# Normalisation, residual and first-projection steps of a three-layer hybrid kernel rearranged

## The reference

```
h = rms_norm(x, g_norm);  proj = h @ w_in              # RWKV-7 scan, conv, memory attention
y = gates0*y_rwkv + gates1*y_conv + gates2*y_mem
x = rms_norm(x + y @ w_out, g_final)
for layer in range(2):
    h = rms_norm(x, norm_pre[layer]);  proj = h @ w_in_2[layer]
    y = concat(gla(...), diff_attention(...), hgrn(...)) @ w_out_2[layer]
    x = x + rms_norm(y, norm_post[layer])
# rms_norm(x, g) = x * rsqrt(mean over channels of x*x, plus 1e-6) * g
```

## Time and profile before

| | us |
|---|---|
| median of three runs | 4637.75 (4632.31 to 4640.51) |
| the profiled execution | 4640.63, its span 4638.7 |
| PE busy | 3902.2 (84%) |
| DVE busy | 2036.1 (44%) |
| ACT busy | 1438.2 (31%) |
| POOL busy | 1007.3 (22%) |

### The profile page before, as it was taken

One profiled execution on the slowest core, in us unless ns is written; L12 is line 12 of the kernel. 1 busy time (PEld: TensorE's weight loads), 2 busy tenths in 40 slices (PEclk: granted clock), 3 DMA queues, 4 the chain that ended last, 5 costly groups with the idle time before them and its releaser, 6 DMA issues.

```text
span 4638.7 us, 66428 instructions
## 1 busy us (share of the span) xinstructions
PE 3902.2 (84%) x29046; PEld 2418.3 (52%) x29346; DVE 2036.1 (44%) x2160; ACT 1438.2 (31%) x1794; POOL 1007.3 (22%) x442
## 2 busy tenths in 40 slices
PE   5988899999989999777995977979685877978776
PEld 2555565665656654345443555555452455555443
DVE  3456455455444551412224254263734254264642
ACT  4222323323233221311113323434443232343442
POOL 2313333233332321111131101111023200111013
PEclk9999999999999999888997988989897978989888
DMA  2111111111111113223222100100011100100011
GB/s 89 51 38 38 52 38 47 47 51 52 38 51 38 51 65 141 77 95 114 104 69 74 33 10 9 42 14 28 19 59 61 33 10 10 41 19 19 23 50 55
DMA packets 61585, 226.93 MB, mean 49 GB/s; under 512 B 6832, under 2 KB 8560, under 8 KB 60784
## 3 DMA queue, kind: packets, MB, share of 16 engines
q1 hardware_dynamic: 50064, 181.77, 11.3%
q10 hardware_dynamic: 11232, 40.90, 2.2%
HBM read 174.93 MB, written 47.71 MB: 48 GB/s over the span
## 4 chain that ended last, share of the span: by engine, by line
PE 68%; DVE 17%; ACT 10%; issue 2%; POOL 2%; DMA 1%; ACTq 0%; DVEq 0%; SPq 0%; POOLq 0%
PE psum L886 66%; DVE arena L1925 6%; ACT arena L1419 6%; DVE arena L1928 5%; DVE arena L2355 2%; DVE arena L2292 2%; POOL arena L2401 2%; PE psum L889 1%; ACT L1419 1%; DVE arena L1932 1%; ACT hh L1419 1%; ACT wh L1419 1%; ACT arena L1866 1%; DVE hl L1925 1%; POOL wl L2401 0%
## 5 line engine op out<-in xcount | busy, mean ns | idle before, releaser
L886 PE MATMUL psum<-arena 64*64 64x32 f32 (+12 forms) x19058 | 1595.4, 284 | 505.9 <-DVE arena L1925 199.8
L886 PEld LDWEIGHTS psum<-arena 64*64 64x64 f32 (+6 forms) x19058 | 1114.5, 160 | 994.4 <-issue 512.3
L2401 POOL TENSOR_TENSOR wl<-arena,wh 128x1024 bf16<-128x1024 f32 (+1 forms) x195 | 474.7, 2435 | 2436.2 <-ACT wh L1419 2434.2
L886 PE MATMUL psum<-hh,wh 128*128 128x512 f32 x3120 | 890.3, 432 | 121.8 <-ACT hh L1419 72.9
L1419 ACT ACTIVATE arena<-psum 128x512 f32<-128x512 f32 (+4 forms) x660 | 415.8, 630 | 1242.5 <-PE psum L886 960.2
L886 PEld LDWEIGHTS psum<-hh,wh 128*128 128x128 f32 x3120 | 609.0, 201 | 330.6 <-ACT hh L1419 85.1
L1925 DVE TENSOR_TENSOR arena<-psum,arena 128x512 f32<-128x512 f32 (+3 forms) x488 | 319.4, 654 | 980.0 <-PE psum L886 635.1
L886 PE MATMUL psum<-hh,wl 128*128 128x512 bf16 (+1 forms) x2911 | 727.9, 392 | 20.7 <-issue 7.4
L886 PE MATMUL psum<-hl,wh 128*128 128x512 bf16 (+1 forms) x3029 | 717.6, 383 | 10.6 <-issue 8.1
L1928 DVE SCALAR_TENSOR_TENSOR arena<-arena 128x1024 f32<-128x1024 f32 (+1 forms) x388 | 610.1, 1572 | 118.4 <-ACT arena L1419 103.4
L1925 DVE TENSOR_TENSOR arena<-arena 128x1024 f32<-128x1024 f32 (+9 forms) x514 | 434.3, 845 | 371.2 <-ACT arena L1419 209.2
(11 more groups left out here) (30 smaller groups left out, 819.5 us busy)
## 6 DMA issues: line engine op xcount, KB each, us to landing
arena<-in_w_in SPq DMA_DIRECT2D x161, 512.0 KB, 3.5
scr_g<-arena ACTq DMA_DIRECT2D x24, 512.0 KB, 2.6
arena<-scr_g SPq DMA_DIRECT2D x24, 512.0 KB, 4.6
arena<-in_w_out SPq DMA_DIRECT2D x24, 512.0 KB, 3.5
arena<-in_w_mem_kv SPq DMA_DIRECT2D x16, 512.0 KB, 3.5
scr_x<-arena SPq DMA_DIRECT2D x16, 512.0 KB, 2.6
arena<-scr_x SPq DMA_DIRECT2D x16, 512.0 KB, 7.3
arena<-in_x SPq DMA_DIRECT2D x8, 512.0 KB, 10.3
```

Source lines behind the costliest of these rows:

```text
L886: return pe.e.matmul(o, l, r, start=start, stop=stop)
L2401: return pool.seq.tensor_tensor(o, a, b, op)
```

## The change

- The inverse root of every norm stays in PSUM: Ln and Exp work in place on the statistics' pair of banks, and DVE reads it there. The pair is given back by the last norm (or the last residual multiplication), not by Ln.
- `stat_sum`: PE multiplies the sum of the first seven slices by ones, then the eighth's squares by ones into the same banks. The last `stat_add` is gone and four passes are added. For `pre1` there is no `stat_add`: PE sums every slice's squares (`stat_mm`).
- `resid`: DVE multiplies all eight slices; DVE adds the even ones and POOL the odd ones. For layer 0 it runs inside the `pre1` statistics, and `stat_sq` k waits for slice k alone.
- `ahead_by_two`: the plan says norm k, then split k-2; `norm_pre` has four rotating buffers.
- In `post0`/`post1` `stat_sq` comes ahead of `close`, and `close` gives back the projection's banks.
- The low parts of `m0` and `m1` are all made by DVE.
- The first projections named in `EARLY` go slice by slice: for each k the two high x high matmuls and the two with the weights' low part, and at the end the 16 with the activations' low part.

```diff
@@ stat, ahead_by_two (plan)
         for k in range(8):
+            if tag == "pre1":
+                do("resid", 0, k)
             do("stat_sq", tag, k)
-            if k:
+            if tag == "pre1":
+                do("stat_mm", tag, k)
+            elif 0 < k < 7:
                 do("stat_add", tag, k)
             yield
-        do("stat_sum", tag)
-        ps.leave(("stat", tag))
+        if tag != "pre1":
+            do("stat_sum", tag)
         do("stat_end", tag)
+    def ahead_by_two(norms, tag):
+        for k in range(10):
+            if k < 8:
+                do(*norms[k])
+            if k > 1:
+                do("split", tag, k - 2)
-    for k in range(8):
-        do("norm_x", k)
-        do("split", "h", k)
+    ahead_by_two([("norm_x", k) for k in range(8)], "h")
+    ps.leave(("stat", "x"))
@@ closing (plan)
-            do("close", tag, ct)
+            if tag == "fin":
+                do("close", tag, ct)
             do("stat_sq", tag, ct)
-            if ct:
+            if 0 < ct < 7:
                 do("stat_add", tag, ct)
+            if tag != "fin":
+                do("close", tag, ct)
@@ the two layers (plan)
-        for k in range(8):
-            do("norm_pre", L, k)
-            do("split", f"p{L}", k)
+        ahead_by_two([("norm_pre", L, k) for k in range(8)], f"p{L}")
+        ps.leave(("stat", f"pre{L}"))
...
-        for ct in range(NT):
-            do("resid", L, ct)
+    for ct in range(NT):
+        do("resid", 1, ct)
@@ PE
+    EARLY = [("lo", 0), ("m", 1, 0), ("fin", 0)]
+    EARLY += [("dvp", 0, 0), ("sv", 0, 0, 0), ("post0", 0), ("dvp", 1, 0), ("sv", 1, 0, 0), ("post1", 0)]
+    def lo_by_dve(tag, k):
+        return 1 if tag[0] == "m" else k % 2
-                kind, c0, k = q // each, q % each // 8 * 512, q % 8
+                if key in EARLY:
+                    kind, c0, k = (q % 4 // 2, q % 2 * 512, q // 4) if q < 32 else (2, q % 2 * 512, q % 16 // 2)
+                else:
+                    kind, c0, k = q // each, q % each // 8 * 512, q % 8
@@ PE, stat_sum
-            pe.wait_ge(*at("stat_add", tag, 7))
+            pe.wait_ge(*at("stat_add", tag, 6))
             for c in range(0, n, 512):
                 e = min(n, c + 512)
-                x = mm(o[:, c:e], ones, stat_acc(tag)[:, c:e])
+                mm(o[:, c:e], ones, stat_acc(tag)[:, c:e], True, False)
+            pe.wait_ge(*at("stat_sq", tag, 7))
+            for c in range(0, n, 512):
+                e = min(n, c + 512)
+                x = mm(o[:, c:e], ones, STAT[tag][2][1][:, c:e], False, True)
             x.then_inc(*pe.up("stat_sum", tag))
+        def stat_mm(tag, k):
+            pe.wait_ge(*at("stat_sq", tag, k))
+            src = STAT[tag][2][k % 2] if k else stat_acc(tag)
+            for c in (0, 512):
+                x = mm(o[:, c:c + 512], ones, src[:, c:c + 512], k == 0, k == 7)
@@ ACT
             elif tag == "pre1":
-                act.wait_ge(*at("resid_pool", 0, 7))
-                act.wait_ge(*at("resid_dve", 0, 6))
+                act.wait_ge(*at(("resid_dve", "resid_pool")[k % 2], 0, k))
-            f(rs[:, 0:n], pair(("stat", tag))[:, 0:n], AF.Ln, bias=EPS6, scale=1.0 / D).then_inc(*act.up("stat_ln", tag))
-            ps.give(("stat", tag), ("stat_ln", tag))
-            f(rs[:, 0:n], rs[:, 0:n], AF.Exp, scale=-0.5).then_inc(*act.up("stat", tag))
+            f(inv_root(tag), inv_root(tag), AF.Ln, bias=EPS6, scale=1.0 / D).then_inc(*act.up("stat_ln", tag))
+            f(inv_root(tag), inv_root(tag), AF.Exp, scale=-0.5).then_inc(*act.up("stat", tag))
@@ DVE (norm_x, mem_norm and norm_fin alike)
-            if k > 1:
-                dve.wait_ge(*ready_h(f"p{L}", k - 2))
-            stt(sl(1024 * (k % 2), 1024), XR[:, k, :], V("norm_pre_2", 8 * L + k), STAT[f"pre{L}"][3], MUL, MUL).then_inc(*dve.up("norm_pre", L, k))
+            if k > 3:
+                dve.wait_ge(*ready_h(f"p{L}", k - 4))
+            stt(sl(1024 * (k % 4), 1024), XR[:, k, :], V("norm_pre_2", 8 * L + k), inv_root(f"pre{L}"), MUL, MUL).then_inc(*dve.up("norm_pre", L, k))
+            if k == 7:
+                ps.give(("stat", f"pre{L}"), ("norm_pre", L, 7))
         def resid(L, ct):
+            dve.wait_ge(*at("stat", f"post{L}"))
+            dve.wait_ge(*at("close", f"post{L}", ct))
+            tt(BB[:, ct, :], BB[:, ct, :], inv_root(f"post{L}"), MUL).then_inc(*dve.up("resid_mul", L, ct))
             if ct % 2 == 0:
                 dve.wait_ge(*at("xr_in", L))
                 tt(XR[:, ct, :], XR[:, ct, :], BB[:, ct, :], ADD).then_inc(*dve.up("resid_dve", L, ct))
@@ POOL
             if ct % 2:
-                pool.wait_ge(*at("stat", f"post{L}"))
                 pool.wait_ge(*at("xr_in", L))
-                tt(BB[:, ct, :], BB[:, ct, :], STAT[f"post{L}"][3], MUL).then_inc(*pool.up("resid_mul_pool", L, ct))
+                pool.wait_ge(*at("resid_mul", L, ct))
                 tt(XR[:, ct, :], XR[:, ct, :], BB[:, ct, :], ADD).then_inc(*pool.up("resid_pool", L, ct))
```

More of the change, by code:

```diff
@@ L573, in memory @@
         do("mem_norm")
+        ps.leave(("stat", "mem"))
         for ct in range(8):
@@ L828, in build @@
     for stage, names in (
-            ("weights", "load proj split"), ("stat", "stat_sq stat_add stat_sum stat_end norm_x norm_fin norm_pre close resid"),
+            ("weights", "load proj split"), ("stat", "stat_sq stat_add stat_mm stat_sum stat_end norm_x norm_fin norm_pre close resid"),
             ("keys", "init shift lo_tanh ksq ksum kn kn2 lora_load lora lsig cs kh rkh bsum powers bon ar bk"),
@@ L1338, in do_sum @@
             sums(("do_sum", L, h), "sums", ones, PX)
-        does = dict(proj=proj, vmp=vmp, stat_sum=stat_sum, ksum=ksum, lora=lora, bsum=bsum, G=g_mats, vt=vt, sx=sx, sp=sp,
+        does = dict(proj=proj, vmp=vmp, stat_sum=stat_sum, stat_mm=stat_mm, ksum=ksum, lora=lora, bsum=bsum, G=g_mats, vt=vt, sx=sx, sp=sp,
                     sq=sq, ta=ta, bt=bt, w0=w0, tu=tu, mr=mr, dd=dd, y0=y0, ch=ch_step, ys=ys, gmean=gmean, gvar=gvar, usum=usum, usqs=usqs, ms=ms, mt=mt,
@@ L1368, in stat_acc, with inv_root @@
         return acc[:, 0:n]
+    def inv_root(tag):
+        return pair(("stat", tag))[:, 0:STAT[tag][0]]
     final = {}
@@ L1383, in split_src @@
         if tag[0] == "p":
-            return sl(1024 * (k % 2), 1024)
+            return sl(1024 * (k % 4), 1024)
         return BA[:, k, :]
@@ L1455, in stat_sq @@
             if k > 2:
-                act.wait_ge(*at("stat_add", tag, k - 2))
+                act.wait_ge(*at("stat_mm" if tag == "pre1" else "stat_add", tag, k - 2))
             elif tag == "mem":
@@ L1715, in close @@
             f(BB[:, ct, :], pair(("proj", (tag, ct))), AF.Copy, scale=V("norm_post_2", 8 * L + ct)).then_inc(*act.up("close", tag, ct))
+            ps.give(("proj", (tag, ct)), ("close", tag, ct))
         def small(L):
@@ L1949, in norm_x @@
             dve.wait_ge(*at("stat", "x"))
-            stt(BC[:, k, :], BC[:, k, :], V("g_norm", k), STAT["x"][3], MUL, MUL).then_inc(*dve.up("norm_x", k))
+            stt(BC[:, k, :], BC[:, k, :], V("g_norm", k), inv_root("x"), MUL, MUL).then_inc(*dve.up("norm_x", k))
+            if k == 7:
+                ps.give(("stat", "x"), ("norm_x", 7))
         def split(tag, k):
-            if k % 2:
+            if lo_by_dve(tag, k):
                 dve.wait_ge(*at("hi", tag, k))
@@ L2174, in mem_norm @@
             for k in range(8):
-                x = stt(MT[:, k, :], MT[:, k, :], V("g_mem_norm", k), STAT["mem"][3], MUL, MUL)
+                x = stt(MT[:, k, :], MT[:, k, :], V("g_mem_norm", k), inv_root("mem"), MUL, MUL)
                 x.then_inc(*(dve.up("mem_norm") if k == 7 else dve.up("mem_norm", k)))
+            ps.give(("stat", "mem"), ("mem_norm",))
         def ms(h, b):
@@ L2207, in norm_fin @@
             dve.wait_ge(*at("stat", "fin"))
-            stt(BC[:, ct, :], BC[:, ct, :], V("g_final", ct), STAT["fin"][3], MUL, MUL).then_inc(*dve.up("norm_fin", ct))
+            stt(BC[:, ct, :], BC[:, ct, :], V("g_final", ct), inv_root("fin"), MUL, MUL).then_inc(*dve.up("norm_fin", ct))
+            if ct == 7:
+                ps.give(("stat", "fin"), ("norm_fin", 7))
         def norm_pre(L, k):
             dve.wait_ge(*at("stat", f"pre{L}"))
-            if k > 1:
-                dve.wait_ge(*ready_h(f"p{L}", k - 2))
-            stt(sl(1024 * (k % 2), 1024), XR[:, k, :], V("norm_pre_2", 8 * L + k), STAT[f"pre{L}"][3], MUL, MUL).then_inc(*dve.up("norm_pre", L, k))
+            if k > 3:
+                dve.wait_ge(*ready_h(f"p{L}", k - 4))
+            stt(sl(1024 * (k % 4), 1024), XR[:, k, :], V("norm_pre_2", 8 * L + k), inv_root(f"pre{L}"), MUL, MUL).then_inc(*dve.up("norm_pre", L, k))
+            if k == 7:
+                ps.give(("stat", f"pre{L}"), ("norm_pre", L, 7))
         def small(L):
@@ L2414, in split @@
         def split(tag, k):
-            if k % 2 == 0:
+            if not lo_by_dve(tag, k):
                 pool.wait_ge(*at("hi", tag, k))
```

13 lines of the change are left out of this document (7 added, 6 removed).

## The result

The changed kernel takes 4565.24 us (median of four runs, 4556.62 to 4578.9); the kernel before took 4635.95 (4632.31 to 4640.51) beside it. The ratio is 0.985, 95% interval 0.9822 to 0.9877: faster by 1.2 to 1.8%. The forecast was 4576.0, range 4558 to 4594. Twice more beside other kernels it gave 4578.58 (ratio 0.9868, 0.9836 to 0.9899) and 4571.33 (0.9859, 0.9838 to 0.9879). One execution in this document, of the kernel with `EARLY` off, took 5922.55 us at a granted clock of 0.632 and is left out of that kernel's median and ratio.

A forecast was written before the change was run, and what follows sets the result against it. PE was taken as the bound, with the gain in the seams where it waits for vector work. Terms from +1.7 to -20.9 us summed to -61.7, off the median 4637.75: 4576.0 us, range 4558 to 4594.

The forecast's parts named there:

- Start: First norm-and-split stretch: Ln of x +1.5 us later, then first norm to the end of `lo` -8.2 us.
- rival C: `p0` and `p1`: low parts, not high ones, end last, so the gain is 2 us each; 4583 us, chance 0.10.
- the bound on cooling: fin's first tile: -0.5 us, bounds -1.5 to +2, since waits between low parts may cool PE.
- `p0`, `p1`: Layers' projections after the first norm: end at 38.1 us against 43.5, -5.4 us each, bounds -3.4 to -9.
- The new wait on n7: `p0` and `p1`: PE stands at `sv`'s first matmul until the eighth norm returns the statistics' PSUM pair, at 17.0 us.
- Rivals A: Start, `p0`, `p1`, residuals: much milder stretching, eighth norm at 13 us; about -17 us, 4559 us, chance 0.13.
- `m0`, `m1`: Layers' closings: 20 matmuls instead of 41 after the eighth high part, DVE's low parts just in time; -6.2 us each.
- The weight DMAs: `m0` and `m1`: costed at nothing; a late DMA at the third tile would give back 4 us.
- One of the prediction's own signs of being wrong: `m0`: PE matmuls showing 0.45 us each would mean the prediction is wrong.
- Residual, `pre1`, end: From `post0` through the residual to Ln of `pre1`, -20.9 us; the end of the kernel, -9.1 us.
- Rival B: Thin stretches: PE stays at half clock; `pre1` sums +7 us, `m0` and `m1` +4 each; 4593 us, chance 0.12.
- Rival D: Steady parts: PE fills its gaps and is granted less clock; 2% gives 4654 us, slower than before; chance 0.02.

The follow-up runs named there:

- the kernel with the norms ahead: Changed kernel with all eight norms ahead of all splits on DVE, each in its own buffer: 4551.19 us, ratio 0.9813 to the kernel before.
- run 32: Not a run or kernel: in "let PE run 32 matmuls" the word run is a verb and 32 counts matmuls.
- The upper half: Changed kernel with the sums of `pre0` and `pre1` in the upper half of PSUM, so `sv` needs no pair from it: 4558.45 us, ratio 0.9827.
- the three edits together: Changed kernel with `pre0`/`pre1` sums in upper PSUM, low parts of y on DVE alone, all norms ahead of splits: 4531.72 us, ratio 0.9789.
- the last two runs: The changed kernel with upper-PSUM sums, y low parts on DVE and norms ahead, 4531.72 us; and the changed kernel unedited a third time, 4571.33 us.

## Why the prediction was right

**What bounds it, and that the seams pay in full.** Right. PE's busy time stayed, and -59.5 of -61.6 us lie in the seams, -59.8 of -58.4 and -60.2 of -64.5 in the two repeats.

**Start.** The sum was +1.3 for +1.5. n7 ended 17.1 after the first norm for 17.0, the eighth high part 18.2 for 18.1, from the rule that a low part that meets POOL's ends 1.08 after it. Of the tail the prediction took the middle between 4.6 us at the fast and 9 at the slow clock. PE ran the last 20 matmuls from 49.12 to 55.86 without a wait, 6.7 us; the granted clock was 0.50 to 0.52 until 53.3 and 1.00 from there. So the size (-7.8 for -8.2) and the reason were right. DVE's last two low parts, stretched, end at 54.40, and PE comes to the eighth slice's only at 55.26: rival C's mechanism, low parts that end last, has 0.9 us to spare here, and the kernel with the norms ahead shows it in `lo`.

```profile
45.22 2.60 DVE L1968 SCALAR_TENSOR_TENSOR arena<-arena,psum 128x1024 f32<-128x1024 f32 x2
47.92 6.48 DVE L1965 TENSOR_TENSOR hl<-arena,hh 128x1024 bf16<-128x1024 f32 x2
...
49.18 1.42 PE L909 MATMUL psum<-hh,wh 128*128 128x512 f32 x2
50.40 1.08 PE L909 MATMUL psum<-hh,wl 128*128 128x512 bf16 x2
51.27 4.59 PE L909 MATMUL psum<-hl,wh 128*128 128x512 bf16 x15
...
55.90 1.11 ACT L1463 ACTIVATE arena<-psum,arena 128x1024 f32<-128x1024 f32 x1 [5.84 <-PE psum L909]
```

**fin.** The first tile and the sum were right. The step that failed is the bound on cooling, "-1.5 to +2" counted for the first tile alone: PE's waits for POOL's low parts, the longest 2.24 us, slow the second tile too, which the earlier trace rows didn't show. The granted clock was 1.00 until 2390, 0.50 from 2392.3 to 2401.1 and 0.97 after. These rows tell it, sixteen matmuls in 6.21 where the third tile's take 4.01:

```profile
2392.32 1.89 PE L909 MATMUL psum<-hl,wh 128*128 128x512 bf16 x4 [2.24 <-POOL hl L2451]
2395.60 1.89 PE L909 MATMUL psum<-hl,wh 128*128 128x512 bf16 x4 [1.39 <-POOL hl L2451]
2396.93 6.21 PE L909 MATMUL psum<-hh,wh 128*128 128x512 f32 x16
```

So `EARLY` loses 1.5 us at fin, +2.0 - 0.5, where the kernel without it shows both the old times. The loss isn't steady: the changed kernel's two repeats lose 0.2 and 1.0. In the first of them PE's waits are the same to 0.01 us, but the clock is back at 1.00 about 3 us sooner. The old order let PE run 32 matmuls of the other products while POOL finished.

**`p0`, `p1`.** The new wait on n7 was found, with its length: PE goes on at 17.3 for 17.0 and needs 21.4 for 21.1. The upper half took it away and gave 20.1 in the time. Of the 0.8 that is missing in `p0`, 0.23 is an edge ('s window is 43.5, the stretch by instructions 43.27), 0.27 the later n7 and 0.3 the tail. Rivals A and C did not come: the low parts s1 and s3 took 3.20 and 3.18 us, and n7 ended at 17.2, not 13; the low parts end 21.9 us after the first norm and hold nothing.

**`m0`, `m1`.** -6.07 and -6.08 for -6.2. Both halves were needed: the order alone, with POOL's share back, loses 3.9 and 2.5; the old order loses 6.0. The weight DMAs that were costed at nothing cost nothing. One of the prediction's own signs of being wrong did appear, matmuls at 0.43 us in `m0`: the granted clock was 0.53 from 3429.4 to 3432.6, behind PE's wait of 2.35 us for the first high part. It cost little: a high part came only every 1.1 us, and PE reached the eighth slice 0.5 us after its high part.

**Residual, `pre1`, end.** -21.5 for -20.9 and -9.3 for -9.1. Rival B's clock didn't come: the first twelve passes of `pre1` took 8.13 us, at half clock until about 3531, the next eight 3.70, at a granted clock of 1.00, and it stayed there through waits of 0.37 to 1.07 us. The Trainium skill's "TensorE: Matmul & The Clock Gate", section on HAM oscillation, describes a loop that starts every burst slow after waits for transfers of several microseconds. The residual's waits are much shorter than those, so its rows don't contradict the page; what they contradict is the prediction's reading of it for this loop. The stretch that decided it is the overlap of sums and residual, 14.1 us.

**PSUM as a source.** No price: 1220 to 1222 ns for the multiplications, 5.23 for four norms as with SBUF. The larger fixed cost that the Trainium skill gives PSUM sources ("VectorE: DVE Perf Modes", TRN2 errata) doesn't show in these rows. The prediction had the gain of the PSUM root within the residual and the norms; taken alone it is 11.7 us in the kernel's time.

**How close it came.** The sum, -61.7, was worked out on a profiled run, and the profiled run came 61.6 shorter. That agreement to 0.1 is luck: the seams gave 2.2 us less than the sum, by fin's second tile (+2.0) and `p0` and `p1` (+1.5) less what other terms gained, and the mixers and merges happened to give 2.0. Against the sum the seams came 1.5 to 2.2 us short in all three profiles. The medians differ by 70.7, 58.8 and 63.9 on three occasions; what varies lies in the mixers and merges. There is only one profile of the kernel before (mixers 873.5 and 873.8), so no run shows whether the change has a part in that.

**Rival D** (a lower clock in the steady parts) didn't come. The mean clock of a whole run counts the seams too, so the mixers are the test: 867.72 and 861.84 us in the kernel with the fullest seams, the three edits together, against 873.45 and 873.81 before.

## What to carry to other kernels

Where the engine with the most work idles in seams, price each seam by a timeline of vector operations, down to which of them meet another engine's; such sums held within a microsecond here, except around fin, where waits of up to 2.24 us let the clock fall. After a reordering look for the buffer that is given back last: the largest remaining gain, 20 us, was a PSUM pair held by the statistics' root, and moving it was one word. An operand in PSUM kept VectorE from being stretched beside GpSimd (1.22 us against up to 3.25 for 128x1024), and giving a second engine half of a short queue can cost more than it brings (2.5 to 3.9 us in each closing).

## What the runs showed of the hardware that was not expected

- GpSimd is slowed as well: three of its four additions take 3.33 to 3.38 us beside VectorE multiplications from SBUF, all four 2.35 beside those from PSUM.
- ScalarE reads and writes PSUM in 1.09 us (Ln, 128x1024) and 1.01 (Exp), no more than into SBUF (1.11).
- TensorE slowed down at fin though none of its waits was over 2.24 us: after waits of 1.27 and 2.24 with four matmuls between, the granted clock was 0.50 for 8.8 us. Nearly equal waits don't always do the same: behind 0.59 and 2.25 us the last low parts of `lo` ran fast in one kernel, behind 0.61 and 2.25 slow in another.
- Layer 0's mixer takes 865 to 869 us in five of the eleven profiles of the changed kernel and its edits, and 874 to 879 in six; the kernel before has 873. Four of the five short ones are those of one chip, but on the chip of the last two runs one was short (867.7) and one long (878.7), so neither the chip nor the edit alone explains it. In the pairs of profiles above the difference goes with the granted clock, 0.93 or 0.89 in a sixth of the mixer, 1.00 or 0.93 in a piece of the merges. What decides which is granted was not found.
